# An output projection begun before the layer norm, and its end, the norm behind it and the first MLP pair split by token halves

## The reference, cut to what matters

```
attn_x = neighbourhood_attention(...)                 # 512 features
conv_x = silu(layer_norm(conv(...)) * ln_g + ln_b)    # 512 features
x_new = x + g1 * (concat([attn_x, conv_x]) @ w_out)   # 1024 x 1024
hx2 = modulate(rms_norm(x_new, norm2_g), sh2, sc2)
x_new = x_new + g2 * (square(relu(hx2 @ w_mlp1)) @ w_mlp2)   # hidden 4096
```

## Time and profile before

| what | value |
|---|---|
| median of 3 runs | 2692.78 us (2683.35 to 2696.69) |
| the profiled execution's own time | 2692.5 us |
| its span from first to last instruction | 2690.4 us |
| TensorE busy | 2532.0 us, 94% |
| VectorE, ScalarE, GpSimd busy | 1314.0, 755.1, 865.7 us |
| mean granted TensorE clock | 0.975 |

### The profile page before, as it was taken

How to read it: one execution, slowest core, us unless ns; L and a number is a source line. 1 busy time by engine, 2 the same in 40 slices (tenths; PEclk the granted TensorE clock), 3 DMA queues, 4 the chain that set the end, 5 groups by cost and what they waited for, 6 DMA issues and landing times.

```text
span 2690.4 us, 33826 instructions
## 1 busy us (share of the span) xinstructions
PE 2532.0 (94%) x13640; PEld 2062.0 (77%) x13640; DVE 1314.0 (49%) x1303; ACT 755.1 (28%) x1140; POOL 865.7 (32%) x380
## 2 busy tenths in 40 slices
PE   5999888897999999999989989999999999999999
PEld 3788677586887878878767678888888877777877
DVE  4799688535444444444484767841023221343131
ACT  4201277504121111211244367731000110241010
POOL 1343300033444435344423200024444434514332
PEclk8999899998999999999989999999999999999999
DMA  6111465210111111111121100001111111202112
GB/s 252 40 40 55 123 178 179 98 47 32 47 54 41 55 40 55 47 48 47 48 94 40 32 1 1 1 32 47 62 48 55 48 40 55 64 31 110 47 40 86
DMA packets 54841, 165.64 MB, mean 62 GB/s; under 512 B 5348, under 2 KB 23912, under 8 KB 53288
## 3 DMA queue, kind: packets, MB, share of 16 engines
q1 hardware_dynamic: 49008, 140.68, 16.2%
q10 hardware_dynamic: 5688, 22.81, 2.2%
HBM read 152.98 MB, written 10.49 MB: 61 GB/s over the span
## 4 chain that ended last, share of the span: by engine, by line
PE 84%; DVE 8%; ACT 3%; issue 2%; DMA 2%; POOL 1%; SPq 0%; ACTq 0%; DVEq 0%; POOLq 0%
PE region L272 24%; PE region L274 24%; PE region L273 24%; PE pv L1546 2%; PE aux L1536 2%; PE pv L349 1%; DVE conv L1031 1%; ACT na_prob L921 1%; DVE tmp L425 1%; PE aux L358 1%; PE pv L887 1%; DVE h_lo L419 1%; DMA rs_again<-rs_spill 1%; DVE x L1844 1%; DVE na_prob L962 1%
## 5 line engine op out<-in xcount | busy, mean ns | idle before, releaser
L1924 POOL TENSOR_TENSOR w_hi<-w_raw,der 128x1024 fp32r<-128x1024 f32 x186 | 362.0, 1946 | 1787.7 <-PE region L274 1742.2
L272 PE MATMUL region<-h_hi,w_hi 128*128 128x512 f32 x1760 | 693.7, 394 | 43.7 <-DVE h_lo L419 20.7
L274 PE MATMUL region<-h_hi,w_lo 128*128 128x512 f32 x1760 | 689.6, 392 | 0.0
L273 PE MATMUL region<-h_lo,w_hi 128*128 128x512 f32 x1760 | 689.5, 392 | 0.0
L1927 POOL TENSOR_TENSOR w_lo<-w_raw,w_hi 128x1024 fp32r<-128x1024 f32 x186 | 503.1, 2705 | 14.6
L272 PEld LDWEIGHTS region<-h_hi,w_hi 128*128 128x128 f32 x1760 | 333.6, 190 | 114.7 <-issue 41.0
L273 PEld LDWEIGHTS region<-h_lo,w_hi 128*128 128x128 f32 x1760 | 333.7, 190 | 76.2 <-issue 8.0
L274 PEld LDWEIGHTS region<-h_hi,w_lo 128*128 128x128 f32 x1760 | 333.1, 189 | 70.4
L272 PE MATMUL region<-ff_hi,w_hi 128*128 128x512 f32 x512 | 199.2, 389 | 0.0
L273 PE MATMUL region<-ff_lo,w_hi 128*128 128x512 f32 x512 | 199.2, 389 | 0.0
L274 PE MATMUL region<-ff_hi,w_lo 128*128 128x512 f32 x512 | 199.2, 389 | 0.0
(11 more groups left out here) (332 smaller groups left out, 3858.7 us busy)
## 6 DMA issues: line engine op xcount, KB each, us to landing
w_raw<-units SPq DMA_DIRECT2D x186, 512.0 KB, 3.5
w_raw<-w_ada_late SPq DMA_DIRECT2D x32, 512.0 KB, 4.3
bias<-na_bias SPq DMA_DIRECT2D x24, 384.0 KB, 3.8
ada_buf<-w_ada SPq DMA_DIRECT2D x4, 2048.0 KB, 13.5
x_sb<-x_t ACTq DMA_DIRECT2D x2, 2048.0 KB, 13.7
v_pair<-v_spill SPq DMA_DIRECT2D x64, 64.0 KB, 3.3
x<-x_t ACTq DMA_DIRECT2D x1, 4096.0 KB, 13.5
x_spill<-x ACTq DMA_DIRECT2D x1, 4096.0 KB, 11.4
```

What stands on the lines that cost most here:

```text
L272: pe.matmul(dst, wh, xh, start=first, stop=False)
L273: pe.matmul(dst, wh, xl, start=False, stop=False)
L274: return pe.matmul(dst, wl, xh, start=False, stop=last)
L1924: pool.tensor_tensor(w_hi[:, s], w_raw[:, s], one_col.broadcast_to([P, 1024]), ALU.mult)\
```

## The change

1. Out1's units 0 and 1 do their blocks 0 to 3 (attention) early: unit 0 ahead of the layer norm's mean sums, unit 1 between these and the variance sums (`out1_blocks`). After the norm `out1_pe` does blocks 4 to 7 of both, one k at a time, unit 0 then unit 1.
2. The variance sums run with the feature block outside and the token quarter inside.
3. The barrier between the layer norm and out1 is gone.
4. The last unit of out1 signals after its first half of the tokens (`out1_part`). The RMS norm is done by halves: squares, sums, root, inverse and spread of the first half lie between matmuls of that unit's second half (`beside`), those of the second half behind it. The norm's blocks are 128x512 with a ring of four slots.
5. The first pair of every MLP group goes through `project_pair_by_halves`: the LAGGED order over the first half of the tokens, then again over the second.
6. Semaphores of the attention stages are shared (`KINDS`, `COUNTS`), which alters names and wait values and no order.

```diff
@@ def project @@
+                if beside is not None and lo:
+                    beside(k)
...
+            if half_done is not None and lo == 0:
+                last.then_inc(half_done, 1)
...
+    def project_pair_by_halves(pe, arrive, xh, xl, wait_hk):
+        for h in range(2):
+            t = slice(h * HALF, h * HALF + HALF)
+            for n, k in LAGGED:
+                if h == 0 and k == 0:
+                    arrive(n)
+                if n == 0:
+                    wait_hk(h, k)
+                w = slice(k * P, k * P + P)
+                last = mm3(pe, region[:, n, t], w_hi[:, n, w], w_lo[:, n, w], xh[:, k, t], xl[:, k, t], k == 0, k == KD - 1)
+                if h and k == KD - 1:
+                    last.then_inc(unit_done, 1)
...
     def ln_variance_pe(e):
         reach(e, "ln_dev", 4)
-        for q in range(4):
-            for j in range(4):
-                if q == 0:
-                    reach(e, "ln_sq", j + 1)
+        for j in range(4):
+            reach(e, "ln_sq", j + 1)
+            for q in range(4):
...
+    def out1_blocks(e, pos, n, a, b):
+        if a == 0:
+            e.wait_ge(unit_split, UNIT0["out1"] + n + 1)
+            wait_region(e, pos.use + n)
+        for k in range(a, b):
+            if k >= 4 and n == 0:
+                reach(e, "lnn_lo", k - 3)
...
+            if k == KD - 1:
+                last.then_inc(unit_done, 1)
...
-        start_pair(e, pos, UNIT0["out1"], mix_hi, mix_lo, lambda k: reach(e, "lnn_lo", k - 3) if k >= 4 else None)
+        for k in range(4, KD):
+            for n in range(2):
+                out1_blocks(e, pos, n, k, k + 1)
+        pos.use += 2
+
+        def beside(k):
+            if k == 2:
+                r2_sums_pe(e, 0)
+            if k == KD - 1:
+                r2_spread_pe(e, 0)
+
         for j in range(2, 8):
             use = pos.next_use()
-            project(e, use, UNIT0["out1"] + j, mix_hi, mix_lo, KD).then_inc(unit_done, 1)
+            last = j == 7
+            project(e, use, UNIT0["out1"] + j, mix_hi, mix_lo, KD, half_done=sem("out1_part") if last else None,
+                    beside=beside if last else None).then_inc(unit_done, 1)
+        r2_sums_pe(e, 1)
+        r2_spread_pe(e, 1)
...
+        last(0)
+        inverse(0)
+        for i in range(2 * KD):
+            h, k = divmod(i, KD)
+            t = slice(h * HALF, h * HALF + HALF)
+            if k == 0:
+                reach(e, "r2_spread", h + 1)
+            if i >= 4:
+                reach(e, "n2_lo", i - 3)
+            e.tensor_tensor(n2_slots[:, i % 4], x1[:, k, t], pv[:, h], ALU.mult).then_inc(sem("n2_nm"), 1)
+            if i == 0:
+                last(1)
+            if i == 1:
+                low(0)
+            if i == 2:
+                inverse(1)
+            if i >= 3:
+                low(i - 2)
...
-            project_pair(e, arrive, h2_hi, h2_lo, lambda k: reach(e, "n2_lo", k + 1))
+            project_pair_by_halves(e, arrive, h2_hi, h2_lo, lambda h, k: reach(e, "n2_lo", KD * h + k + 1))
...
             na_pe(pe, pos)
             tell()
+            reach(pe, "na_lo", NA_N)
+            out1_blocks(pe, pos, 0, 0, 4)
             ended(1)
             ln_mean_pe(pe)
+            out1_blocks(pe, pos, 1, 0, 4)
             ln_variance_pe(pe)
-            tell()
             out1_pe(pe, pos)
-            r2_pe(pe, pos)
             mlp_pe(pe, pos)
```

More of the change, by code:

```diff
@@ L89 @@
     "rms": [("r1", 8), ("rc", 8), ("rm", 8)],
-    "norm": [("n1", 8), ("nc", 8), ("lnn", 4), ("n2", 8), ("n3", 8), ("nq", 3), ("nk", 2), ("nm", 8)],
-    "att": [("ma", 32)],
+    "norm": [("n1", 8), ("nc", 8), ("lnn", 4), ("n2", 16), ("n3", 8), ("nq", 3), ("nk", 2), ("nm", 8)],
+    "att": [("na", 0), ("mla", 0), ("ma", 0)],
     "gate": [("ga", 4), ("gm", 4)],
@@ new lines, in r2_sums_pe, with r2_spread_pe @@
+    def r2_sums_pe(e, h):
+        reach(e, "r2_acc", 6)
+        reach(e, "r2_sq", 8 + h)
+        for q in range(4):
+            t = slice(h * HALF + q * P, h * HALF + (q + 1) * P)
+            rows = slice(32 * q, 32 * q + 32)
+            e.matmul(aux[rows, h * HALF:h * HALF + P], ones[:, 0:32], tmp[:, 2, t], start=True, stop=False)
+            last = e.matmul(aux[rows, h * HALF:h * HALF + P], ones[:, 0:32], tmp[:, 1, t], start=False, stop=True)
+        last.then_inc(sem("r2_sqmm"), 1)
+    def r2_spread_pe(e, h):
+        reach(e, "r2_rs", h + 1)
+        for q in range(4):
+            pick = ident[:, 32 * q:32 * q + 1].broadcast_to([P, P])
+            last = e.matmul(pv[:, h, q * P:(q + 1) * P], pick, tmp[:, 3, h * P:(h + 1) * P], start=True, stop=True)
+        last.then_inc(sem("r2_spread"), 1)
@@ L1090, in out1_dve @@
     def out1_dve(e, pos, ch):
         reach(e, "x_again", 16)
-        for j in range(8):
+        for j in range(7):
             use = pos.next_use()
@@ L1102, in out1_dve, with last, low, inverse @@
                 e.tensor_tensor(tmp[:, 2], tmp[:, 2], tmp[:, j % 2], ALU.add).then_inc(sem("r2_acc"), 1)
+        use = pos.next_use()
+        def last(h):
+            if h:
+                e.wait_ge(unit_done, UNIT0["out1"] + 8)
+            else:
+                reach(e, "out1_part", 1)
+            t = slice(h * HALF, h * HALF + HALF)
+            e.scalar_tensor_tensor(out=x1[:, 7, t], in0=region[:, use % 2, t], scalar=mod_x[:, 23:24],
+                                   in1=x1[:, 7, t], op0=ALU.mult, op1=ALU.add).then_inc(sem("r2_half"), 1)
+            if h:
+                reach(e, "r2_half", 2)
+                e.sem_inc(free[use % 2], 1)
+        def low(i):
+            h, k = divmod(i, KD)
+            t = slice(h * HALF, h * HALF + HALF)
+            reach(e, "n2_hi", i + 1)
+            e.tensor_tensor(h2_lo[:, k, t], n2_slots[:, i % 4], h2_hi[:, k, t].bitcast(F32), ALU.subtract).then_inc(sem("n2_lo"), 1)
+        def inverse(h):
+            inverse_dve(e, "r2", h + 1, tmp[:, 3, h * P:(h + 1) * P])
+        last(0)
+        inverse(0)
+        for i in range(2 * KD):
+            h, k = divmod(i, KD)
+            t = slice(h * HALF, h * HALF + HALF)
+            if k == 0:
[11 more added lines that the diff above has]
+                low(i - 2)
+        low(2 * KD - 2)
+        low(2 * KD - 1)
+        reach(e, "n2_lo", 2 * KD)
+    n2_slots = place("n2_slots", [4, HALF], 165)
     def out1_act(e, pos, ch):
-        for j in range(8):
+        for j in range(7):
             use = pos.next_use()
@@ L2112, in _ @@
             tell()
-            ended(4)
+            ended(3)
             mla_pe(pe, pos)
@@ L2125, in _ @@
             tell()
-            ended(10)
+            ended(9)
             mem_att.pe(pe, pos)
```

51 lines of the change are left out of this document (36 added, 15 removed).

## The result

| what | before | after |
|---|---|---|
| median | 2693.19 us (20 runs, 2683.35 to 2696.69) | 2697.39 us (20 runs, 2692.15 to 2701.01) |
| profiled execution, its span | 2692.5, 2690.4 us | 2692.15, 2690.4 us |
| VectorE, ScalarE, GpSimd busy | 1314.0, 755.1, 865.7 us | 1311.0, 757.6, 871.8 us |

The ratio is 1.0016 [1.0009, 1.0022]. That is slower by a sixth of a per cent, and no change by the bound of half a per cent. The medians lie 4.2 us apart; the prediction said 2697.0, by +4.5.

A forecast was written before the change was run, and what follows sets the result against it. The prediction took TensorE, busy for 2532 of 2690.4 us, to bound the kernel. Its terms 8.2 + 0.6 - 7.3 + 3.0 = +4.5 us on 2692.5 gave 2697.0 us, range 2685 to 2707.

The forecast's parts named there:

- the class: Whole kernel: no change within half a per cent (13.5 us), chance 0.86; faster 0.05, slower 0.09.
- The waits ahead of unit 2: MLP first pairs: TensorE waits for GpSimd 2.99 us instead of 0.27, 2.72 us more in each group.
- Start of out1: Layer norm to out1's unit 2: later mean sums, cheaper variance sums, new wait for GpSimd; +0.6 us, bounds -2.9 and +4.4.
- the spread: Layer norm, after root and inverse: counted at 2.48 us.
- End of out1 and RMS norm: Out1's unit 7 to the MLP's unit 2: norm by halves starts the MLP earlier; -7.3 us, bounds -11.4 and -2.9.
- the first low part: RMS norm's block 0 on VectorE, while GpSimd splits: counted at 1.5 us, or 3.0 by the lock-out rule.
- Groups 1 to 3: MLP groups after the first: GpSimd's lost cover costs 3 x 2.72 = +8.2 us, lower bound 0.
- nothing is won: MLP groups 1 to 3: the input has long been there, so halving the pair gains no time.
- The clock: Behind five new TensorE waits of 3.0 to 3.5 us: two drops at 1.5 us, +3.0 us, bounds 0 and 12.
- the waits don't appear: Rival: no TensorE waits for GpSimd ahead of unit 2; -12.9 us, 2679.6 us, chance 0.07.
- the clock falls at each of the five waits: Rival: half-level clock behind all five new TensorE waits; +13.5 us, 2706.0 us, chance 0.13.

The follow-up runs named there:

- experiment 4, e3_halves_only: The kernel before with only each MLP group's first pair by halves, the norm still in blocks of all tokens: 2718.5 us, ratio 1.0097.
- experiments 8 to 10: The changed kernel with four, eight and twelve drain instructions on TensorE ahead of the MLP loop: 2699.89, 2698.3 and 2699.64 us, one run each.
- the kernel before with a fast turn: The kernel before with eight drain instructions, which compute nothing, on TensorE ahead of the MLP loop: 2682.24 us, ratio 0.9962.
- e9_after_pad4: The changed kernel with four drain instructions on TensorE ahead of the MLP loop: 2699.89 us, one run.
- e11_after_pad12: The changed kernel with twelve drain instructions on TensorE ahead of the MLP loop: 2699.64 us, one run.
- e10_after_pad8: The changed kernel with eight drain instructions on TensorE ahead of the MLP loop: 2698.3 us, one run.
- e6_reordered: Changed kernel with longer head and tail in MLP first pairs, mean sums first, early blocks in the layer norm's waits, out1's unit 0 ending earlier: 2667.67 us, ratio 0.9902.

## Why the prediction was right, and where it was right by luck

The time and the class were right, 2697.0 against 2697.39 us. Step by step:

- **The waits ahead of unit 2** in the MLP were right in place, cause and size: 2.76 us four times, 2.66 us more per group than before where 2.72 was predicted, released by GpSimd's second pass.
- **Start of out1**, predicted +0.6, measured +1.58: from attention's output to unit 2 it takes 552.01 - 504.17 = 47.84 us instead of 549.56 - 503.30 = 46.26. The chain came out as worked: mean sums late by 5.3 us, the variance sums at 1.94 us (2.2 predicted), an idle time of 5.00 us, a wait for GpSimd of 3.19 us. The mis-sized term is the spread, counted at 2.48 us: it came behind 2.38 us of idle time at the half clock (granted 0.50 from 528 to 530 us) and took 3.66.
- **End of out1 and RMS norm**, predicted -7.3, measured -8.3. The path to the MLP's first matmul came out as worked: it starts 73.93 us behind out1's unit 2 (625.94 - 552.01), and 623.6 - 549.56 = 74.0 was predicted. The 1.0 us lies behind it, where 7 matmuls ran at the half clock and 12 were counted. One term on that path was mis-sized without showing in the sum: the first low part, at 621.30, met GpSimd's pass (619.75 to 621.64) and took 0.88 us, not the 1.5 us counted, where undisturbed ones take 0.69. The Trainium skill (SBUF — State Buffer, on the shared port pair) has the later of the two wait out the other's whole instruction. Here only 0.34 us of that were left, and 0.88 us is no longer than such a wait would make it, so the changed kernel neither shows the rule wrong nor lets it cost much.
- **Groups 1 to 3**, predicted +8.2, measured +10.8 with the clock in it. Two terms were missed here. The turn of the loop, in the earlier trace rows as 2.76 us of "issue", was taken as fixed and gave back 8.0 us. And the sentence that the input has long been there and so "nothing is won" holds the silent assumption that the only cover at stake is that of unit 2. The shorter order also takes the cover of unit 1's own weights, which share a buffer with the last unit of the group before: 12 matmuls lie ahead of its first one instead of 24, for GpSimd's 4.3 us. That is +1.91 three times, +5.7 us, but only since the turn is fast: experiment 4, with the slow turn that the prediction reckoned with, doesn't have these waits.
- **The clock** was counted at two drops of five, +3.0. In the profiled execution it fell at all four waits of the MLP and not at out1's, at 1.6 us each: +6.4 (three of them in the 10.8 above, the fourth behind group 3's unit 2). The earlier trace rows had shown 2.76 us without a drop, and experiments 8 to 10 have three to five drops at the same five waits. So the length of the wait alone doesn't decide, the count changes from execution to execution, and nothing here shows what decides. The Trainium skill (TensorE: Matmul & The Clock Gate, HAM oscillation) warns of just this repeated return; the trace agrees with its direction, at gaps of 2.76 us.

So the errors, +5.7 and +3.4 against -8.0, nearly cancel, and the right total is in part luck: the fast turn, which nothing in the prediction called for, gives 8.0 us and takes 5.7 of them back. At the MLP's end they leave the changed kernel 5.6 us behind, by the sum of the steps, where +4.5 was predicted; the medians say 4.2. The order's true price is seen with the turn equal: the kernel before with a fast turn runs in 2682.24 us, 15.2 us less than the changed kernel. Of these, 8.2 are the turn inside the MLP and 5.6 what the steps cost; the remaining 1.4 us are less than these medians can tell.

The chance on "the waits don't appear" was for a case that didn't come; "the clock falls at each of the five waits" came for four of five in the profiled execution, at 1.6 us each instead of the 2.4 counted. It came whole in the run of e9_after_pad4, which took 2699.89 us and not 2706.

## What to carry to other kernels

Before a pair is interleaved more finely, or halved, ask for each buffer it uses how many matmuls stand between the release and the next need, at the pair's head as well as at its tail; here 12 matmuls instead of 24 cost 2.7 us at the tail of each pair and, where the loop's turn is fast, 1.91 us at its head, and a longer tail alone gave 15.5 us. Work that can be done early belongs into the waits of the chain, behind its first step and not ahead of it: here the 48 early matmuls cost time with half of them ahead of the mean sums, and with all of them behind, and a longer tail, the pair ended 9.7 us earlier. And before two versions of a loop are compared, look at the duration of the loop's branch in both, and at the packets of the instruction queue: the turn differed by some 3 us with no difference in the loop's own code, and a version may owe its rank to that.

## What the hardware showed that was not expected

TensorE's backward branch over the MLP's loop took 0.21 us or 3.35 to 3.9 us, in kernels with the same instructions at the loop's end: slow in the kernel before, with 1 drain ahead, and with the halves alone; fast with 4 or 8 drains, in the changed kernel and in all seven made from it. That the place of the loop in TensorE's list decides is shown by the drains. With the slow branch goes a loading of instructions in each pass (117 packets in the instruction queue against 91); which places bring it on stays open.

The clock behind short idle times differed between executions at the same place. Behind out1's 3.19 us it was full in the changed kernel and at 1.2 GHz for some 12 matmuls in e9_after_pad4 and e11_after_pad12. Behind the 2.76 us ahead of unit 2 it fell for 7 to 9 matmuls most times, but not in group 0 of e10_after_pad8 and e11_after_pad12, nor in groups 0 and 2 of e3_halves_only. At the slow turn it stayed full in the kernel before (2.4 to 2.8 us idle) and with 1 drain (up to 3.07 us), and fell in e3_halves_only (2.7 to 2.8 us). It fell behind 2.26 us in e6_reordered and never behind the waits of 1.75 us. The count of such drops is thus worth a range in a forecast, and a difference of a few us in one execution may be nothing else.
